# The first mixer with heads in pairs: row-half scores, values stationary in 64 columns, rotation by a shuffle, projections among the steps

## What is computed

```python
qa, ka, va, qb, kb, vb, qi, ki, wi, ga, gb = split(h @ w_in)   # 23 tiles of 128 columns and 16 of gates
# branch A: 8 heads of 64, softmax(q k / 8 + bias by distance), causal by chunks of 64
o_a = mixer_a(qa, ka, va, rel_bias)
# branch B: rotation of the first 16 of each head's 64 rows in q, k, qi, ki;
# 8 index heads score the keys, the best 128 of them are kept for each query,
# 8 query heads share 2 key/value heads
o_b = mixer_b(rope(qb), rope(kb), vb, rope(qi), rope(ki), wi)
merged = sigmoid(ga) * (o_a @ w_branch_a) + sigmoid(gb) * (o_b @ w_branch_b)
x = x + merged @ w_out
```

## Time and profile before

| | |
|---|---|
| median of three runs | 2238.59 us |
| profiled execution, its own time | 2236.8 us |
| its span | 2235.0 us |
| mean granted TensorE clock | 0.998 |
| PE, DVE, ACT, POOL busy | 98%, 35%, 35%, 39% |
| first mixer up to its merge | 376 to 738 us of the span |

### The profile page before, as it was taken

One profiled execution on the slowest core, in us unless ns is written; L12 is line 12 of the kernel. 1 busy time (PEld: TensorE's weight loads), 2 busy tenths in 40 slices (PEclk: granted clock), 3 DMA queues, 4 the chain that ended last, 5 costly groups with the idle time before them and its releaser, 6 DMA issues. The chain is left out here.

```text
span 2235.0 us, 27488 instructions
## 1 busy us (share of the span) xinstructions
PE 2196.9 (98%) x9986; PEld 1785.1 (80%) x9986; DVE 771.7 (35%) x1159; ACT 777.8 (35%) x1065; POOL 869.0 (39%) x363
## 2 busy tenths in 40 slices
PE   7999999999999999999999999999999989999999
PEld 6888887766777888888887888888888877888887
DVE  5222212587322342222215222212666655222200
ACT  5222322234433442332323222323565644222221
POOL 4444444331122344444444444444231324444443
PEclk9999999999999999999999999999999999999999
DMA  4322234221111232222332332233111112232332
GB/s 160 102 97 100 94 104 150 78 68 46 39 59 47 85 96 102 94 94 94 104 113 85 103 98 100 94 104 103 48 49 47 48 40 92 94 99 99 101 114 75
DMA packets 56045, 196.53 MB, mean 88 GB/s; under 512 B 6384, under 2 KB 6768, under 8 KB 55984
## 3 DMA queue, kind: packets, MB, share of 16 engines
q1 hardware_dynamic: 54720, 192.93, 26.0%
q10 hardware_dynamic: 1264, 2.75, 0.4%
HBM read 193.43 MB, written 2.10 MB: 87 GB/s over the span
## 5 line engine op out<-in xcount | busy, mean ns | idle before, releaser
L305 POOL TENSOR_TENSOR w_lo<-raw,w_hi 128x1024 fp32r<-128x1024 f32 x359 | 868.8, 2432 | 1347.1 <-ACT w_hi L697 1345.6
L331 PE MATMUL ps<-xn_hi,w_hi 128*128 128x512 f32 x1912 | 762.5, 399 | 19.5 <-DVE xn_lo L996 8.6
L333 PE MATMUL ps<-xn_hi,w_lo 128*128 128x512 f32 x1912 | 747.2, 391 | 0.0
L332 PE MATMUL ps<-xn_lo,w_hi 128*128 128x512 f32 x1912 | 746.9, 391 | 0.0
L331 PEld LDWEIGHTS ps<-xn_hi,w_hi 128*128 128x128 f32 x1912 | 360.2, 188 | 129.9 <-issue 36.9
L333 PEld LDWEIGHTS ps<-xn_hi,w_lo 128*128 128x128 f32 x1912 | 360.0, 188 | 76.6
L332 PEld LDWEIGHTS ps<-xn_lo,w_hi 128*128 128x128 f32 x1912 | 360.6, 189 | 73.6 <-issue 2.4
L697 ACT ACTIVATE w_hi<-raw 128x1024 fp32r<-128x1024 f32 x359 | 364.6, 1047 | 129.4 <-PE ps L333 118.3
L964 DVE TENSOR_TENSOR scratch<-ps,rstd 128x512 f32<-128x512 f32 x207 | 142.7, 691 | 585.7 <-PE ps L333 585.3
L331 PE MATMUL ps<-h_hi,w_hi 128*128 128x512 f32 x704 | 273.9, 389 | 0.0
L332 PE MATMUL ps<-h_lo,w_hi 128*128 128x512 f32 x704 | 273.9, 389 | 0.0
(11 more groups left out here) (179 smaller groups left out, 1702.6 us busy)
## 6 DMA issues: line engine op xcount, KB each, us to landing
raw<-weights SPq DMA_DIRECT2D x359, 512.0 KB, 3.5
x_sb<-x_t SPq DMA_DIRECT2D x8, 256.0 KB, 5.2
bias<-rel ACTq DMA_DIRECT2D x1, 2048.0 KB, 9.6
out_t<-x_sb SPq DMA_DIRECT2D x8, 256.0 KB, 4.7
rope<-ropes ACTq DMA_DIRECT2D x1, 512.0 KB, 3.8
const<-consts SPq DMA_DIRECT2D x1, 192.0 KB, 7.2
to_round<-consts SPq DMA_DIRECT2D x1, 192.0 KB, 7.6
ki<-ki ACTq DMA_DIRECT2D x1, 128.0 KB, 2.2
```

Source lines behind the costliest of these rows:

```text
L305: nc.gpsimd.tensor_tensor(w_lo[s][:, :, :], raw[s][:, :, :], w_hi[s][:, :, :].bitcast(F32), ALU.subtract).then_inc(S["lo_done"], 1)
L331: pe.matmul(to, w_hi[s][:, k, :], hi, start=opens, stop=False)
L332: pe.matmul(to, w_hi[s][:, k, :], lo, start=False, stop=False)
L333: last = pe.matmul(to, w_lo[s][:, k, :], hi, start=False, stop=ends)
```

## The change

The steps are halved in number: one step now has a pair of heads, 32 in all. In branch A the four query blocks of one head pair follow each other; in branch B the four pairs of one query block do. Of a pair, one head's queries and keys lie in rows 0 to 63 and the other's in rows 64 to 127, and their two score matmuls are issued in a row into two banks (scores, L493 of the new file). The row sums are now divided out before the transposes, two DVE operations on the weights per step (normalise, L1224 and L1228). The values are the stationary side, 64 columns of them, and 128 columns of transposed weights move; the two heads' results go to PSUM partitions 0 to 63 and 64 to 127 of one bank (weigh_values, L523). The result needs no transpose back, so L515 goes.

The rotation multiplies by sine and cosine straight from PSUM, moves the sine part by a DVE shuffle (L1129) and subtracts; L445 and its matrix go. The index scores come in 12 pairs, written between the tiles of units 2 to 7 (INDEX_AT). Only 8 units run alone; 15 are laid among the 16 steps of branch A and the 16 gates among branch B, in parts of one k, about 7.5 and 7.1 of them per step, before and behind the transposes. The 48 select rounds stand two at the end of each DVE step from step 0 on. Keys, queries and values of branch A have two buffers instead of four. SP's loads follow the new order of units.

```diff
-PROJ = [(KI, 0)] + [(what, t) for what in (QI, QA, KA, VA) for t in range(4)] + [
+PROJ = [(KI, 0)] + [(QI, t) for t in range(4)] + [(what, t) for t in range(4) for what in (QA, KA, VA)] + [
     (KB, 0), (VB, 0), (QB, 0), (QB, 1), (QB, 2), (QB, 3)]
-PROJ_ALONE = 17
+PROJ_ALONE = 8
...
-INDEX = [(i, h) for i in range(1, QT) for h in range(HEADS)]
-INDEX_FROM, INDEX_EACH = 6, 3
+STORED = {KI: 0, QI: 1, QA: 5, KA: 9, VA: 13, KB: 17, VB: 18, QB: 19}
...
+INDEX = [(t, i) for t in range(4) for i in range(1, QT)]
+INDEX_AT = [(2, 7), (3, 2), (3, 6), (4, 2), (4, 6), (5, 2), (5, 5), (6, 1), (6, 4), (6, 7), (7, 2), (7, 5)]
 ROUNDS = TOPK // 8
-TOP_FROM, TOP_EACH = 8, 4
-STEPS = [(br, i, h) for br in range(2) for i in range(QT) for h in range(HEADS)]
+TOP_EACH = 2
...
+STEPS = [(0, i, c) for c in range(4) for i in range(QT)] + [(1, i, c) for i in range(QT) for c in range(4)]
 HALF = len(STEPS) // 2
+HEADS_OF = [[(2 * c, 2 * c + 1) for c in range(4)], [(c, 4 + (c ^ 1)) for c in range(4)]]
...
+        def turn_values_1(n):
+            v = VALUES.index(n)
+            pe.wait_ge(S["v_made"], v + 1)
+            for i in range(QT):
+                last = pe.transpose(PS[:, 7, P * i:P * (i + 1)], v_flat[:, P * i:P * (i + 1)], ident)
+            last.then_inc(S["v_turned"], 1)
+        def between(t):
+            for g in range(filled(t - 1), filled(t)):
                 n, k = divmod(g, UK)
                 u = unit_between(n)
                 if k == 0 and n >= 2:
                     pe.wait_ge(*evacuated_between(n - 2))
+                elif k == 0:
+                    pe.wait_ge(*evacuated_1(PROJ_ALONE + n - 2))
                 unit(u, u % NSLOT, [2 + n % 2] * UK, xn, part=(k, k + 1))
+        def scores(m):
+            br, i, c = STEPS[m]
+            q, k = ((qa, ka[:, c % 2, :]), (qb, kb))[br]
+            if br == 0 and i == 0:
+                pe.wait_ge(S["plain_made"], 2 * c + 2)
+            if br == 1 and i == 0:
+                pe.wait_ge(S["rope_added"], 7 + (c | 1))
+            if m:
+                pe.wait_ge(S["s_biased"], 2 * m)
+            for a in range(2):
+                rows = slice(HD * a, HD * a + HD)
+                t = c % 2 if br == 0 else HEADS_OF[1][c][a] % 4
+                pe.matmul(PS[:, 4 + a, 0:P * (i + 1)], q[rows, t, P * i:P * (i + 1)],
+                          k[rows, 0:P * (i + 1)], start=True, stop=True).then_inc(S["s_done"], 1)
+        def turn_weights(n):
...
+        def turn_weights(n):
+            br, i, c = STEPS[n]
+            for a in range(2):
+                pe.wait_ge(S["p_normed"], 2 * n + a + 1)
+                if n:
+                    pe.wait_ge(S["pt_copied"], 2 * n - 1 + a)
+                for j in range(i + 1):
+                    last = pe.transpose(PS[:, 6 + a, P * j:P * (j + 1)],
+                                        scratch[:, 2 * (n % 2) + a, P * j:P * (j + 1)], ident)
+                last.then_inc(S["p_turned"], 1)
+        def weigh_values(n):
+            br, i, c = STEPS[n]
+            group, e = divmod(n, 4)
+            pe.wait_ge(S["pt_copied"], 2 * n + 2)
+            if e == 0:
+                if group >= 2:
+                    pe.wait_ge(S["o_lo_done"], group - 1)
+                pe.wait_ge(S["v_copied"], min(group, 4) + 1)
+            for j in range(i + 1):
+                for a in range(2):
+                    h = HEADS_OF[br][c][a]
+                    cols, to = slice(HD * a, HD * a + HD), slice(HD * (h % 2), HD * (h % 2) + HD)
+                    at = P * (e if br == 0 else h // 2)
+                    v = va[:, c % 2, j, cols] if br == 0 else vb[:, j, cols]
+                    last = pe.matmul(PS[to, group % 2, at:at + P], v, p_t[:, a, P * j:P * (j + 1)],
+                                     start=(j == 0), stop=(j == i))
+            last.then_inc(S["pv_done"], 1)
         def attention_1():
-            pe.wait_ge(S["plain_made"], 8)
-            pe.wait_ge(S["relu_done"], len(INDEX))
+            pe.wait_ge(S["relu_done"], 2 * len(INDEX))
             for m in range(LAST_STEP + 1):
+                if m >= 2:
+                    weigh_values(m - 2)
                 if m < len(STEPS):
-                    br, i, h = STEPS[m]
-                    t, r = (h // 2, HD * (h % 2)) if br == 0 else (h % 4, HD * (h // 4))
-                    q = (qa, qb)[br][r:r + HD, t, P * i:P * (i + 1)]
...
-                    k = ka[r:r + HD, t, 0:P * (i + 1)] if br == 0 else kb[r:r + HD, 0:P * (i + 1)]
-                    if br == 1 and i == 0 and h < 4:
-                        pe.wait_ge(S["rope_added"], 7 + h)
-                    if m >= 2:
-                        pe.wait_ge(S["s_biased"], m - 1)
-                    pe.matmul(PS[:, 4 + m % 2, 0:P * (i + 1)], q, k, start=True, stop=True)\
-                      .then_inc(S["s_done"], 1)
-                between(m)
-                if m == 0:
-                    turn_1(PROJ_ALONE - 1)
+                    scores(m)
+                for n in turned_in(m):
+                    turn_values_1(n)
+                between(2 * m)
                 if 1 <= m <= len(STEPS):
-                    n = m - 1
-                    br, i, h = STEPS[n]
-                    pe.wait_ge(S["p_made"], n + 1)
-                    if n >= 1:
-                        pe.wait_ge(S["pt_copied"], n)
-                    for j in range(i + 1):
-                        last = pe.transpose(PS[:, 6, P * j:P * (j + 1)],
-                                            scratch[:, 2 + n % 2, P * j:P * (j + 1)], ident)
-                    last.then_inc(S["p_turned"], 1)
-                if 2 <= m < len(STEPS) + 2:
-                    n = m - 2
-                    br, i, h = STEPS[n]
-                    group = n // HEADS
-                    pe.wait_ge(S["pt_copied"], n + 1)
-                    if h == 0 and group >= 2:
-                        pe.wait_ge(S["o_lo_done"], group - 1)
-                    if n in (0, HALF):
-                        pe.wait_ge(S["v_copied"], 5 if n else 4)
-                    for j in range(i + 1):
-                        v = va[:, j, HD * h:HD * (h + 1)] if br == 0 else vb[:, j, HD * (h // 4):HD * (h // 4 + 1)]
-                        last = pe.matmul(PS[:, group % 2, HD * h:HD * (h + 1)],
-                                         scratch[:, 4, P * j:P * (j + 1)], v,
-                                         start=(j == 0), stop=(j == i))
-                    last.then_inc(S["pv_done"], 1)
-                if m % HEADS == 3 and m > HEADS:
-                    g = m // HEADS - 1
-                    pe.wait_ge(S["o_normed"], g + 1)
-                    for c in range(4):
-                        last = pe.transpose(PS[:, g % 2, P * c:P * (c + 1)],
-                                            ssq[:, P * c:P * (c + 1)], ident)
-                    last.then_inc(S["o_turned"], 1)
-                if m - 2 in ENDS and ENDS.index(m - 2) < len(PROJ) - PROJ_ALONE:
-                    turn_1(PROJ_ALONE + ENDS.index(m - 2))
+                    if turned_in(m - 1) or turned_in(m):
+                        pe.wait_ge(S["v_copied"], VALUES.index((turned_in(m) or turned_in(m - 1))[-1]) + 1)
+                    turn_weights(m - 1)
+                between(2 * m + 1)
         def merge():
             pe.wait_ge(S["o_lo_done"], GROUPS - 1)
...
+        def round_group(g):
+            act.wait_ge(S["pv_done"], 4 * g + 4)
+            if g < QT:
+                dst, src = o_hi[0][:, g, :], PS[:, g % 2, :]
+            else:
+                dst = o_hi[1][:, :, P * (g - QT):P * (g - QT + 1)]
+                src = PS[:, g % 2, :].rearrange("p (c n) -> p c n", c=4)
+            copy(dst, src).then_inc(S["o_hi_done"], 1)
         def attention_1():
...
+        def turn_by_angle(n, bank, factor):
             what, t = PROJ[n]
-            return {KI: ki[0:HD, :], QI: qi[:, t, :], KB: kb[:, :], QB: qb[:, t, :]}[what]
-        def finish_rope(n):
-            if n not in ROPE:
-                return
             k = ROPE.index(n)
-            rows = rope_rows(n)
-            dve.wait_ge(S["swap_done"], k + 1)
-            multiply(scratch[rows, 6, :], PS[rows, 7, :], rope[rows, 1, :]).then_inc(S["rope_sined"], 1)
+            rows = slice(0, HD if what == KI else P)
+            turned = {KI: ki[0:HD, :], QI: qi[:, t, :], KB: kb[:, :], QB: qb[:, t, :]}[what]
+            if k == 0:
+                dve.wait_ge(S["tables_scaled"], 2)
+            else:
+                dve.wait_ge(S["rope_turned"], k)
+            scale_two(scratch[rows, 5, :], PS[rows, bank, :], factor, rope[rows, 1, :]).then_inc(S["rope_sined"], 1)
+            scale_two(turned, PS[rows, bank, :], factor, rope[rows, 0, :]).then_inc(S["rope_cosed"], 1)
+            if k:
+                dve.wait_ge(S["rope_added"], k)
             dve.wait_ge(S["rope_sined"], k + 1)
-            nc.vector.tensor_tensor(rope_out(n), rope_out(n), scratch[rows, 6, :], ALU.add)\
-                .then_inc(S["rope_added"], 1)
```

(41 more changed lines are left out.)

372 lines of the change are left out of this document (166 added, 206 removed).

## The result

The changed kernel takes 2183.09 us (median of 4, 2182.13 to 2184.83) against 2238.59; the ratio is 0.9751 with an interval of 0.9737 to 0.9764. The forecast was 2177 in a range of 2169 to 2195. Its profiled execution took 2183.03 us with a span of 2181.2 at a mean granted clock of 0.997, so against the profiled execution before (2236.8) 53.8 us went, of 60 forecast.

A forecast was written before the change was run, and what follows sets the result against it. The prediction took PE's instruction time as the bound. Gains of 10.6 + 26.9 + 7.8 + 13.1 + 4.3 = 62.7 us, less 3 of waits, about 60, took 2236.8 to 2177 us; 8-in-10 range 2169 to 2195.

The forecast's parts named there:

- Bound and mechanism: Whole kernel: PE's instruction time sets the span, so work leaving PE leaves the span if DVE keeps up.
- rotation: First mixer: ten rotation matmuls of 1.01 us and a PE wait of 0.5 go, gain 10.6 us.
- index scores: First mixer: 8 groups of three costing 20.2 us become 12 pairs costing 12.4, gain 7.8 us.
- score pairs and values: Attention steps: paired scores gain 26.9 us; paired 64-column value matmuls, with a third change of shape, gain 13.1.
- transposing back: Attention results: four transposes taking 0.54 us, eight times, all go, gain 4.3 us.
- waits of the mixer: First mixer: new PE waits, in selecting steps and at the first value tile, taken as 3 us in all.
- The second score is free: Score pairs in opposite row halves: two matmuls cost what one does, gain 26.9 us.
- 64-column tiles overlap: Value matmuls: two column halves overlap as row halves do, 0.213 us a pair, 17.1 for 80 pairs.
- the rival without overlap: Value matmuls: 64-column tiles don't overlap, values cost 39.1 us in place of 22.1, time 2194; chance 0.14.
- Price of a change of shape: Between stream, values and scores: 0.155 us each; the third change per step costs 5.0 us over 32 steps.
- the 0.78 at which nothing would be left: Rival at borders of values, scores and stream: 96 costly shape changes, no gain from 0.78 us each; chance 0.03.
- All these windows are at a granted clock of 1.00: Profile windows read before the change: PE's granted clock is 1.00, that is 2.4 GHz.

The follow-up runs named there:

- e4: Changed kernel with one projection tile (three matmuls) between the two score matmuls of a pair: 2211.25 us.
- e8: Changed kernel with softmax weights stationary and 64 columns of values moving, one head after the other, result not transposed back: 2194.01 us.
- e10: Changed kernel plus one unused full-precision matmul over 512 columns behind each of the first five projection units: 2184.55 us.
- e3: Changed kernel with all value matmuls of one head issued before those of the other, no longer alternating column halves: 2186.19 us.
- e6: Changed kernel with one projection tile between a step's values and its scores, four changes of shape instead of three: 2187.14 us.
- e1: Changed kernel with the turning of the index weights two tiles later: 2181.95 us.
- e2: Changed kernel with the turning of the index weights seven tiles later, in unit 2, DVE's copy one unit later: 2183.61 us.
- e9: Changed kernel with index weights turned in unit 2, index pairs up to two tiles later, first value tile turned behind its step's projection tiles: 2178.56 us.
- e7: Changed kernel with scores issued ahead of values in each step: 2183.07 us.
- e11: e9 with the rotation's last operation reading the projection from PSUM, cosine left out: five executions from 2175.49 to 2181.36 us, ratio 0.9737.

## Why the prediction was right, and where 6 us went

**Bound and mechanism: right.** PE's busy time and the span fell together. The parts gave together what they were said to give, 60.7 of 62.7, none of them a fifth less:

| term | forecast | measured |
|---|---|---|
| rotation | 10.6 | 9.7 |
| index scores | 7.8 | 7.5 |
| score pairs and values | 26.9 + 13.1 | 40.0 |
| transposing back | 4.3 | 3.5 |
| waits of the mixer | -3 | -3.8 |
| slow stretch behind a wait | 0 | -1.6 |
| rest of the part | 0 | -0.2 |
| start and end of the part | 0 | -1.3 |
| sum | 60 | 53.8 |

The first four rows are sums over all blocks of the two timelines. The times split the third: parting the scores costs 28.2 (e4, for forecast 26.9), the old form of the values 10.9 (e8, for 13.1). The transposing back was read too dear. In the earlier trace rows its 0.54 runs up to a score's start, and scores start late; two equal blocks of before, with these four transposes and without, tell it:

```profile
608.61 0.40 PE L333 MATMUL ps<-xn_hi,w_lo 128*128 128x512 f32 x1
610.41 0.39 PE L332 MATMUL ps<-xn_lo,w_hi 128*128 128x512 f32 x1
...
504.23 0.40 PE L333 MATMUL ps<-xn_hi,w_lo 128*128 128x512 f32 x1
505.59 0.40 PE L332 MATMUL ps<-xn_lo,w_hi 128*128 128x512 f32 x1
```

They cost 610.41 - 0.23 - 608.84 = 1.34 and 505.59 - 0.23 - 504.46 = 0.90, so four transposes are 0.44, eight times 3.5. The rotation's matmul was read the same way, up to a score's start, as 1.01; in a stream it costs 0.86 (e10), in the steps 0.92; ten and the wait make the 9.7.

**The second score is free: right,** shown by e4 (+28.2 for forecast 26.9). It was read off rows that were already there, for another operand shape.

**64-column tiles overlap: right,** 0.215 a pair; the rival without overlap (2194) asked for L523 groups near 1.7, and they are 1.03. e8, which does the old form in the new place, is 10.9 dearer, and e3 shows that the overlap comes from the other half of the columns and not from the wider moving operand.

**Price of a change of shape: mis-sized.** The step that was mis-sized is "0.31 of each score is fixed: ... 0.155 for each". It left out that the first matmul of a new shape already starts late: 653.92 to 654.24 is 0.32 after the stream instead of 0.23, the 0.09 that I did count for the index pairs. Alone, scores have 0.41 fixed and values 0.37 (e6), both together 0.56: 0.19 for each of three changes, where 0.155 had been taken, 3.0 us over 32 steps. It isn't the precision that costs: work in plain single precision over all rows and columns, put into the same stream, has nothing fixed (blocks of two to eight transposes are 0.11 for each transpose, a matmul over 512 columns is 0.86, four times 0.215). The same slip had priced these blocks of before at 53.8 + 35.2 = 89.0 where they sum to 92.5, and those of after at 49.0 where they sum to 52.5. So it fell out of the difference; that both sides were off by as much is luck, since the old blocks have other shapes and numbers of changes. The Trainium skill, TensorEngine Tiling (Array Packing), section Key Properties, has a change of mode drain the engine; if that is the cause, 0.19 is its price here, and in any case it is far from the 0.78 at which nothing would be left.

**Waits: right in sum, wrong in place.** The text counted 3 us in the selecting steps and at the first value tile. The latter came (1.1), the steps had 0.6. The largest, 2.1, is at the start of the mixer, where the text saw none. DVE does there, on its timeline,

```profile
383.67 3.35 DVE L995 RECIPROCAL rstd<-scratch 128x512 f32<-128x512 f32 x1 [4.46 <-ACT scratch L740]
...
387.19 1.22 DVE L988 TENSOR_TENSOR rope<-rope,rstd 128x512 f32<-128x512 f32 x2
...
389.05 0.69 DVE L991 SCALAR_TENSOR_TENSOR scratch<-ps,rstd 8x512 f32<-8x512 f32 x1
```

one chain before anything of the rotation is ready, and PE now arrives sooner. e1 and e2 show that asking later at one place only moves the wait; e9, which asks later everywhere, leaves 0.9 of it.

**Slow stretch: not foreseen.** "All these windows are at a granted clock of 1.00" was true of before and was taken for granted after. A wait of 2 us is then worth up to 3.7. e9 and e10 fit it (no long wait, no slow stretch in this part of the profile), but e3 and e7 had none either, with the wait.

**Subtraction held by POOL: overlooked.** The prediction priced a rotation at four times 0.69. Before, the last step of a rotation (an addition, L1107) already had instances of 2.56 and 2.36 us; I had read only the cheap ones. Six of ten cost 0.2 to 1.8 us more. None of the changed kernel's own waits stands directly behind one of them; in e1, e2 and e9 PE waited for the first, 0.9 to 2.3 us.

**Start and end.** 1.0 of the 1.3 is that the mixer's first projection began later, 376.99 for 375.96; its start lay between 375.9 and 379.1 in the executions profiled, of kernels whose edits all come later. That 1.0 lies within this scatter, so it isn't put down to the change.

The interval of the ratio is ±3 us, so of these terms only the large ones are shown by times; the small ones rest on block costs of profiled executions. What isn't settled is why a wait of 2 us brings the slower clock in some executions and not in others, what a shorter one can do (outside this part there are slow stretches behind less, see below), and where the clock fell in e11's longer ones.

## What to carry to other kernels

Look first for matmuls of half rows or half columns that stand apart in the program: put side by side with the partner of the other half, the second was free here, in plain single precision, while each change of shape in a stream of full matmuls cost 0.19 us. When PE is shortened, follow the chain of the engine that feeds it at the stage's start, and move all the consumers of this chain later together, since moving one only moved the wait here. An operation of DVE with two SBUF operands beside a busy POOL is to be priced by its longest instances, or given a PSUM operand.

## What the runs showed of the hardware

- Behind a wait of PE of 2.1 to 2.3 us the granted clock fell to half (mean 0.57 in a window of 4 us, matmuls 0.43 us apart) for 3.7 us, in some executions and not in others; behind the longest waits of e1 (1.5), e10 (1.2) and e9 (0.9) in this part it didn't. Elsewhere shorter waits had it too: before the change, behind waits of 0.5 and 1.0 in the second attention, matmuls started 0.43 apart from 1803.62 to 1805.75; after it, behind one of 0.85, from 1521.28 to 1522.99. The Trainium skill, TensorE: Matmul & The Clock Gate, section Part 1: The HAM clock gate, has two states, half rate and full rate; spacings of 0.43 and 0.23 agree with it.
- Column halves overlap as row halves do (0.215 for two matmuls over 128 columns of plain single precision, 0.213 for one), both writing one bank, and the partner needn't be the next matmul (e3: two of a side in a row cost nothing, three 0.27, four 0.49).
- A DVE subtraction with two SBUF operands that starts while POOL's runs ends 0.54 to 0.56 us after it, after up to 2.45 us in all (2.77 in e9, over two of POOL's). The mask's shift in place (L1187) was held as well, with only one tensor as operand:

```profile
609.58 2.21 DVE L1187 TENSOR_SCALAR mask<-mask 128x512 f32<-128x512 f32 x1
```

where the same took 0.43 before; POOL's subtraction ran from 609.14 for 2.36. All three of these shifts of a mask met POOL, in the changed kernel and in e11.
- The shuffle of 128x512 took 0.73 us, against 0.69 taken.
